# A late projection shared anew: 48 of 256 tokens fetched by index, their dots and GpSimd's remainders in it

## The reference

```python
q = (xt @ w_q).reshape(T, PEER_HEADS, 2, PEER_D_QUERY // 2)
s = jnp.einsum('thpd,pnd->thpn', q, sub_keys)
...
ub = jnp.take(u, eb, axis=0)
a = jax.nn.gelu(jnp.einsum('td,tkd->tk', xb, ub), approximate=False) * gb
vb = jnp.take(v, eb, axis=0)
return jnp.einsum('tk,tkd->td', a, vb)
```

## Time and profile before

| | |
|---|---|
| time, median of 3 runs | 1720.07 us (1717.35 to 1722.68) |
| the profiled execution's own time | 1716.15 us |
| its span | 1714.3 us |
| mean granted clock | 0.998 |
| busy: TensorE, VectorE, ScalarE, GpSimd | 1689.3, 1456.4, 923.7, 459.5 us |
| read from HBM | 388.12 MB |

### The profile page before, as it was taken

The page is one execution under the profiler, slowest core; times in us unless marked ns, Lnnn a source line. Parts: engine busy times, 40 slices in busy tenths (PEclk is TensorE's granted clock), DMA queues, the critical chain, the costliest instruction groups (busy, mean ns, idle before and its releaser), DMA issues.

```text
span 1714.3 us, 30335 instructions
## 1 busy us (share of the span) xinstructions
PE 1689.3 (99%) x11590; PEld 1584.9 (92%) x11590; DVE 1456.4 (85%) x2651; ACT 923.7 (54%) x1497; POOL 459.5 (27%) x262
## 2 busy tenths in 40 slices
PE   8999999999999999999999999999999999999998
PEld 8888999999999999999888899999999999999996
DVE  6984899989998998889756669999899888888995
ACT  5554554656555555555535455456555555555552
POOL 6730651000001443444003018210000034434530
PEclk9999999999999999999999999999999999999999
DMA  7545556555557899899723246475555588888991
GB/s 252 191 138 185 174 183 224 183 185 185 191 190 259 312 329 340 309 328 363 284 103 123 89 158 222 157 237 175 191 189 185 196 303 327 331 315 319 346 333 48
DMA packets 108497, 392.28 MB, mean 229 GB/s; under 512 B 12353, under 2 KB 12993, under 8 KB 108097
## 3 DMA queue, kind: packets, MB, share of 16 engines
q1 hardware_dynamic: 85248, 307.42, 52.3%
q0 software_dynamic: 19072, 68.23, 10.5%
q10 hardware_dynamic: 4032, 14.68, 2.5%
HBM read 388.12 MB, written 1.05 MB: 227 GB/s over the span
## 4 chain that ended last, share of the span: by engine, by line
PE 76%; DVE 15%; DMA 4%; issue 2%; ACT 1%; SPq 0%; DVEq 0%; ACTq 0%
PE work L636 17%; PE y L755 9%; PE work L639 9%; PE work L755 9%; PE work L678 6%; PE work L760 5%; PE y L760 5%; PE y L746 4%; DMA raw<-v 4%; DVE y L1898 3%; PE y L1062 3%; PE work L696 3%; PE y L724 2%; DVE far_homes L542 2%; PE work L699 1%
## 5 line engine op out<-in xcount | busy, mean ns | idle before, releaser
L542 DVE TENSOR_TENSOR low<-raw,high 128x1024 fp32r<-128x1024 f32 x404 | 497.2, 1233 | 72.2 <-ACT high L1126 68.8
L1126 ACT ACTIVATE high<-raw 128x1024 fp32r<-128x1024 f32 x442 | 464.6, 1052 | 165.8 <-PE work L678 70.6
L636 PE MATMUL work<-xT,high 128*128 128x448 f32 x1408 | 321.7, 370 | 0.9 <-DVE low L542 0.9
L599 POOL DMA_INDIRECT big<-u_rows,picks x64 | 117.5, 1837 | 663.1 <-DVE big L1798 649.3
L636 PEld LDWEIGHTS work<-xT,high 128*128 128x128 f32 x1408 | 251.6, 189 | 18.4 <-DVE low L542 1.2
L1392 ACT ACTIVATE xT<-big 128x224 fp32r<-128x224 f32 x256 | 97.6, 387 | 214.7 <-PE work L760 213.4
L639 PEld LDWEIGHTS work<-xT,low 128*128 128x128 f32 x1408 | 184.0, 191 | 5.5
L678 PE MATMUL work<-xT,high 128*128 128x224 f32 (+1 forms) x1056 | 182.5, 277 | 3.9 <-POOL low L542 2.1
L1126 ACT ACTIVATE far_homes<-raw 128x1024 fp32r<-128x1024 f32 x138 | 144.8, 1055 | 74.4 <-DMA raw<-v 36.3
L639 PE MATMUL work<-xT,low 128*128 128x224 f32 x1408 | 184.0, 273 | 0.0
L599 POOL DMA_INDIRECT big<-v,picks x64 | 133.2, 2082 | 160.2 <-DVE big L1812 131.1
(11 more groups left out here) (243 smaller groups left out, 2942.9 us busy)
## 6 DMA issues: line engine op xcount, KB each, us to landing
raw<-u SPq DMA_DIRECT2D x256, 512.0 KB, 3.3
raw<-v SPq DMA_DIRECT2D x256, 512.0 KB, 5.4
raw<-wq SPq DMA_DIRECT2D x32, 512.0 KB, 3.2
raw<-conv_in SPq DMA_DIRECT2D x14, 512.0 KB, 4.2
aux<-ln_par ACTq DMA_DIRECT2D x9, 512.0 KB, 5.5
raw<-conv_out SPq DMA_DIRECT2D x8, 512.0 KB, 3.3
raw<-mla_out SPq DMA_DIRECT2D x8, 512.0 KB, 4.4
big<-diag ACTq DMA_DIRECT2D x6, 512.0 KB, 4.4
```

Source lines behind the costliest of these rows:

```text
L542: ops.tensor_tensor(low_at(c), raw[:, slot, :], high_at(c).bitcast(F32), ALU.subtract).then_inc(low_made[slot], 1)
L599: nc.gpsimd.indirect_dma_start(out=side_rows[before % SIDE_BUFS], out_offset=None, in_=rows, in_offset=bass.IndirectOffsetOnAxis(ap=pick_i ...
L636: nc.tensor.matmul(both, w_high[:, cols], xT[:, k, :, 0:DT], start=(k == 0), stop=False)
L1126: A(high_at(c), raw[:, slot, :], ACT.Copy).then_inc(high_made, 1)
```

## The change

**Tokens.** 48 tokens are fetched by index, in two sets: tokens 96 to 127 of the second half in 4 groups of 32, and tokens 80 to 95 in 8 groups of 16. Set one needs 32 gathers of u and 32 of v, set two 16 and 16. 208 tokens stay dense, in 26 batches. Each set has its own copy of x, its own sum and its own selector; the copies take 24 small transfers instead of 8. There are four row buffers.

**Late projection.** VectorE makes 36 of the 48 dots there, one a pair from pair 8 to pair 43, between `gate` and `late`; 12 stay in the columns, at blocks 2 to 21, and the 48 weighted sums follow at blocks 26 to 112. From pair 6 on GpSimd makes the first of a pair's two remainders; it waits until the one-hots of the batches in the pairs before are made, and one gather follows it. VectorE makes the second one before the one-hots and no longer between them and their scaling. Batches are spread evenly over pairs 0 to 41.

**Homes.** `yT` lies in a buffer `columns`, which serves as a fourth home of the ring during the late projection (`spare`: every fourth block), and ScalarE rounds a block further ahead. The columns use the far homes from block 76 on instead of 71. The query weights are loaded at blocks 111, 113 and 115.

```diff
-SIDE = 32
+SETS = ((32, 4), (16, 8))
+SIDE = sum(_n for _n, _ in SETS)
 DT = T - SIDE
-SIDE_BUFS = 3
+SIDE_BUFS = (NKEYS - SIDE_ROOM) // 4 - len(SETS)
-PAIR_OF = [_b if _b < DENSE else DENSE + (_b - DENSE) * 7 // 4 for _b in range(BATCHES)]
+PAIR_OF = [_b * (PAIRS - 3) // (BATCHES - 1) for _b in range(BATCHES)]
+POOL_LOWS_FROM = 6
+EARLY_DOTS = 36
+for _d in range(EARLY_DOTS):
+    DOT_PAIRS.setdefault(8 + _d * (PAIRS - 9) // (EARLY_DOTS - 1), []).append(_d)
+def hots_before(pair):
+    return min(BATCHES, 2 + sum(p < pair for p in PAIR_OF))
...
+                for n in range(SIDE_BUFS):
+                    gather(n)
+                for pair in range(POOL_LOWS_FROM, PAIRS):
+                    pool.wait_ge(hots_ok, batches_before(layer) + hots_before(pair))
+                    make_low(pool, nc.gpsimd, u0 + EARLY + 2 * pair + 4)
+                    for d in DOT_PAIRS.get(pair - 1, ()):
+                        gather(d + SIDE_BUFS)
...
-                nc.tensor.matmul(y[:, 2 + m, :], selector, side_sum[:, m * 512:(m + 1) * 512],
-                                 start=False, stop=False)
+                for pick, total in zip(selector, side_sum):
+                    nc.tensor.matmul(y[:, 2 + m, :], pick, total[:, m * 512:(m + 1) * 512],
+                                     start=False, stop=False)
...
-                    make_high(c + RING)
+                    highs_to(min(c + RING + 1, u0 + NKEYS - 1 + RING - 1) if c > u0 + EARLY else c + RING)
...
                     add_cross(layer, pair)
-                    make_low(dve, V, u0 + n + 4)
+                    if pair < POOL_LOWS_FROM:
+                        make_low(dve, V, u0 + n + 4)
                     if b is not None:
                         gate(layer, b)
+                    for d in DOT_PAIRS.get(pair, ()):
+                        side_dot(layer, d)
                     late(layer, pair)
-                    if more:
-                        make_onehots(layer, b + 2)
                     if pair + 1 < PAIRS:
                         make_low(dve, V, u0 + n + 5)
                     if more:
+                        make_onehots(layer, b + 2)
                         scale_onehots(layer, b + 2)
```

More of the change, by code:

```diff
@@ L132 @@
 Y_CHUNKS = 4
-GROW_FROM, GROW_EVERY = 71, 8
+GROW_FROM, GROW_EVERY = 64 * T // DT - 2, 8
 FAR = {}
@@ L164 @@
     far("wq1", _n, _room)
+SPARE = {FIRST[f"u{_layer}"] + _i for _layer in range(DEPTH) for _i in range(EARLY + RING, NKEYS, RING + 1)}
 OUT_LOWS_POOL = [FIRST["conv_out"] + _n for _n in (1, 2, 3, 4, 5, 7)]
-USED_BEFORE = {}
+USED_BEFORE, RING_SLOT = {}, {}
 _last = {}
 for _c in range(_g):
-    _home = ("far", FAR[_c]) if _c in FAR else _c % RING
+    if _c in FAR:
+        _home = ("far", FAR[_c])
+    elif _c in SPARE:
+        _home = "spare"
+    else:
+        _home = min(range(RING), key=lambda slot: _last.get(slot, slot - RING))
+        RING_SLOT[_c] = _home
     if _home in _last and (_c not in FAR or _last[_home] >= _c - 2 * (len(V_FAR) + RING)):
@@ L254, in program @@
         side_hid = sb("side_hid", [P, SIDE_ROWS])
-        yT = sb("yT", [P, KD, DT])
+        spare_at = -(-nc.sbuf_base // 32) * 32
+        columns = sb("columns", [P, 2 * D])
+        spare = nc.alloc_sbuf_tensor_at("spare", [P, 2, D], F32R, offset=spare_at)
+        yT = columns[:, 0:KD * DT].rearrange("p (k t) -> p k t", t=DT)
         work = ctx.enter_context(nc.psum_tensor("work", [P, 4, 512], F32))
@@ L450, in high_at @@
                 return far_homes[:, FAR[c]:FAR[c] + 4, :].rearrange("p b t -> p (b t)")
-            return high[:, c % RING, :]
+            if c in SPARE:
+                return spare[:, 0, :]
+            return high[:, RING_SLOT[c], :]
         def low_at(c):
@@ L603, in gather @@
                     ).then_inc(side_in[before % SIDE_BUFS], 16)
-                for n in range(2 * SIDE_ROWS):
+                for n in range(SIDE_BUFS):
[5 more added lines that the diff above has]
+                        gather(d + SIDE_BUFS)
+                for n in range(EARLY_DOTS + SIDE_BUFS - len(DOT_PAIRS.get(PAIRS - 1, ())), 2 * SIDE_ROWS):
                     gather(n)
@@ L1783, in combine @@
                 before = 2 * SIDE_ROWS * layer
-                step(V.memset(selector, 0.0))
-                for g in range(SIDE_GROUPS):
-                    at = slice(SIDE * g, SIDE * (g + 1))
-                    last = V.tensor_copy(selector[at, SIDE_AT:P], ident[at, at])
+                for i, (n, groups) in enumerate(SETS):
+                    step(V.memset(selector[i], 0.0))
+                    last = V.tensor_reduce(selector[i][:, SET_AT[i]:SET_AT[i] + n],
+                                           ident[:].rearrange("p (g t) -> p t g", t=n), AX.X, ALU.add)
                 last.then_inc(selector_ok, 1)
-                def rows_of(n):
-                    dve.wait_ge(side_in[n % SIDE_BUFS], 16 * (n // SIDE_BUFS + 1))
-                    return side_rows[n % SIDE_BUFS]
-                def side_dot(d):
-                    rows = rows_of(before + d)
-                    if d == 0:
-                        dve.wait_ge(side_x_in, 16 * SIDE_GROUPS * (layer + 1))
-                    V.scalar_tensor_tensor(rows, rows, 1.0, side_x, ALU.mult, ALU.mult,
-                                           accum_out=side_hid[:, d:d + 1]).then_inc(side_used, 1)
                 def side_weighted(d):
-                    n = before + SIDE_ROWS + d
+                    n, total = before + SIDE_ROWS + d, side_sum[set_of(d)]
                     weight = side_hid[:, d:d + 1]
```

74 lines of the change are left out of this document (50 added, 24 removed).

## The result

The changed kernel takes 1779.07 us (median of 4 runs, 1778.75 to 1781.36), the kernel before 1718.99 (4 runs): ratio 1.0349, 95% interval 1.0329 to 1.0369. It is slower by 60 us. The forecast was slower, by 13 us. The profiled execution took 1778.75 us, its span is 1777.0, 62.7 above that of before.

What follows compares the result with a forecast made beforehand. TensorE was taken to bound the kernel. Per layer late projection +22, columns -16.2, early projection -0.5, side sums +2; twice, less 2 for the weights, +12.6 us on 1716.15, set beside the median as 1733 us, range 1707 to 1766.

Steps and rivals of the forecast that it cites:

- What bounds, and the turns: Whole kernel: TensorE sets the time; late projection: VectorE instructions with two SBUF inputs wait for GpSimd's remainder, +22 us a layer.
- The first rival: Late projection: only two remainders exclude each other, dots and one-hots don't wait, TensorE keeps the pace; 1661 us, chance 0.16.
- It starts just when VectorE starts the pair: Late projection: GpSimd's remainder waits for the batch before's one-hots; pairs with one-hots cost 7.45 us, without 4.99.
- The bounds of +14 and +34: Late projection's +22 us a layer: +14 if GpSimd's turn comes 0.2 us earlier, +34 if the sum often lacks cover.
- Columns: Layer's second part: narrower matmuls save 16.2 us a layer, 13.0 from wide ones and 3.2 from narrow ones.
- third rival: Columns: only the wide matmuls get shorter, giving 13.0 us a layer; inside the forecast's range, no chance of its own.
- The weights now start after the last gather, -2 us: First layer's columns: query weights no longer meet gathers on full queues; -2 us, between 0 and -4.7.
- Covered as well: Columns: gathers and stream, about 97 MB in 294 us, 332 GB/s against 413 seen, add no time.
- TensorE-bound late projection: -13.7 forecast: Late projection: shorter matmuls and two batches fewer save 13.7 us a layer if TensorE still sets the pace.
- Early projection, side sums: Early projection -0.5 us a layer, limited by VectorE's choices; side sums into PSUM by two selectors, +2 us a layer.
- The clock: Late projection: TensorE idles 1.8 us in pairs with one-hots, which can hold the half clock; charged nothing.
- second rival: Late projection: as forecast, and the clock falls too, 1.5 us in each of 19 pairs, +57 us; 1790 us, chance 0.04.

Runs made afterwards that it cites:

- e1: Changed kernel, but VectorE makes all remainders of the late projection again and GpSimd only issues gathers there: 1731.47 us.
- e3: Changed kernel with each of the 36 late dots a layer replaced by a VectorE sum over the same row, one SBUF input instead of two: 1707.29 us.
- e5: Changed kernel with the late product before the dot in each pair: 1738.02 us.
- e6_after_v_low: Changed kernel; GpSimd's remainder of a pair also waits for VectorE's last remainder of the pair before: 1757.03 us.
- w_quarter: Changed kernel with a quarter of each of the three query weight loads in layer 0's columns: 1778.69 us.
- s40_six: Changed kernel with 40 tokens by index, all remainders on VectorE, and 6 late dots a layer, against the same with 12: 1726.26 us.
- e2_no_late_dots: Changed kernel with the 36 late dots a layer left out, one column of the fetched rows copied in place of each: 1686.98 us.

## Why the prediction was off, by its own steps

**What bounds, and the turns: right.** TensorE set the time before; with the change VectorE does in the late projection, by turns with GpSimd. Dots wait, instructions with a PSUM operand don't, the late product behind the dot is what TensorE waits for. e1 shows the waiting to be GpSimd's doing, e3 the classing by inputs, e5 what the late product's place behind the dot costs. The first rival (only two remainders exclude each other, 1661 us) is dead.

**"It starts just when VectorE starts the pair": wrong, and the larger part of the miss.** That sentence set the start of GpSimd's remainder. Behind a pair that makes no one-hots nothing holds GpSimd back: its remainder for the next pair was ready straight behind the gather and came into VectorE's remainder of the pair before. Where GpSimd won, VectorE lost 2.8 us in a place in which nothing runs beside it. e6_after_v_low enforces the start that I had assumed and measures 267.4 us, +23.5 on 243.8, where I had forecast +22. So of the 37.6 us in the mean of both layers, 14.1 are the early start: 28 us of the 31 missed. The other 23.5 hold the forecast's turns; how near they come to its +22 may be partly luck, as the half clock (below) is in them too. The bounds of +14 and +34 that I set on this term were about a turn 0.2 us earlier and about cover at the sum, so they couldn't hold it. It was there to be seen in the diff: `hots_before` is the same number for a pair and the next where the first has no batch, so the wait is already met.

**Columns: mis-sized.** I took -13.0 for the wide matmuls: (1.64 - 1.54) / 8 = 12.5 ns, -12.0 a layer. I took -3.2 for the narrow ones by the step from 256 to 224 columns, with 0 as the bound if the weight load sets that pace: it is 0, as in my third rival. That TensorE's weight loads were busy for 291.5 of 302 us there fits it; no run changed the weight load alone. "The weights now start after the last gather, -2 us" was right in its condition and wrong in what follows from it: TensorE's wait grew from 2.04 to 5.49 us. The gathers were not what they met; three loads within 10 us meet the stream at a DMA share of 1.02 (855 to 861 us), and the three quarters of them that w_quarter leaves out cost some 2.9. Of layer 1's 12.0 only 6.0 arrived. TensorE waited for 5.3 us there, 2.1 before: 1.78 of it behind one block that came late from HBM (1676.78), 1.79 instead of 1.10 at the turn to the last blocks. And the granted clock was at half for 6.8 us (from 1677.6 and 1732.2), where it had never been before; that is up to 3.4 us of work, as an estimate. The two make up the 6. "Covered as well", which I said of 332 GB/s, is the step that failed here (97 MB in 294 us are 330): the stage moves 334 GB/s at a DMA share of 0.93, TensorE's waits in it grew from 3.8 and 2.1 us to 7.2 and 5.3, and s40_six shows what a little more does. The 413 that I set against it is the mean of 5 us.

**TensorE-bound late projection: -13.7 forecast.** e2_no_late_dots shows it: 234.5 in the mean for 243.8, -9.3; with 12.5 ns and 0 instead of 13.6 and 3.3, my sum would have been 704 x 12.5 ns + 1.8 = -10.6.

**Early projection, side sums: right**, -0.4 for -0.5 and 1.5 to 1.8 for the two others. **The clock: charged with nothing, and small.** The forecast let TensorE's idle time hold the half clock; the second rival charged 1.5 us for it in each of the 19 pairs with one-hots. It came twice a layer in the late projection, for 3.4 us each, at most 1.7 us of TensorE's work a time, so at most 3.4 us a layer, as an estimate. Whether even that cost time beside a VectorE that sets the pace is not shown. The second rival's 57 us didn't come.

## What to carry to other kernels

Giving VectorE's work to GpSimd pays, as far as these runs show, only where VectorE has, beside it, work with at most one SBUF input; here 38 GpSimd remainders a layer took 43 us of remainders off VectorE and made the stage 24 us longer in the change's order, and brought nothing in the better order (e5_late_first against e1_v_lows). If two engines exclude each other, fix with a semaphore when the second may start, at a place where the first has work that fits beside it, and put what a third engine waits for ahead of the instruction that will wait. Before moving work into a stage with slack in its engines, look at its DMA share: at 0.93, six more gathers of 0.5 MB cost 13 us in one layer and 6.5 in the other.

## What the hardware showed that I had not expected

GpSimd took its turn ahead of its own recorded start. With its next remainder behind a gather, and that remainder's input ready for over 2 us, it beat a VectorE remainder recorded up to 0.62 us earlier, 16 times of 16, and lost from 0.65 us on, 8 times of 8. Where its input had come only 0.14 to 0.51 us before its recorded start it lost at every distance, 7 times of 7 from 0.08 to 1.06 us. The Trainium skill, SBUF — State Buffer, "Who interferes with whom", says that issue order decides who blocks; the rows agree only if GpSimd's issue lies some 0.6 us before the start that the trace records. The trace doesn't show the issue; that an input ready only 0.51 us before wasn't early enough fits it. The e6 run shows what it costs, not how it comes about.

A narrow matmul of 208 columns took the 0.110 us of one of 224, while one of 256 took 0.120: below 224 columns there was nothing to gain.

Reads ran at up to 426 GB/s in a fortieth of the window of 850 to 880 us, and at 0.93 of the DMA engines' time in the mean of the columns with only 334 GB/s. By the Trainium skill, DMA: Bandwidth & Descriptors, "Where 436 GB/s comes from", reads from HBM are held to about 358. The trace differs: the short peak is above that, and so are the 30 us from 780 in the changed kernel, with 362 GB/s at a DMA share of 0.96. No stage's mean of this study is.
